# Two layers' modulation sums, on VectorE, ScalarE and GpSimd instead of in 32-column fp32 matmuls

## The reference, cut to what matters

```python
mod   = silu(c)     @ ada_w + ada_b        # ada_w is (2048, 6144): shift, scale, gate
mod_c = silu(c_ctx) @ ada_w + ada_b
h  = rms_norm(x)   * (1 + scale)   + shift
hc = rms_norm(ctx) * (1 + scale_c) + shift_c
y, yc = mixer(h, hc)
x = x + gate * y;  ctx = ctx + gate_c * yc
```

## Time and profile before

| | us |
|---|---|
| median of 3 runs | 2321.89 (2319.16 to 2322.77) |
| profiled execution, first to last instruction (span) | 2319.5 |
| what lies around the span, median less span | 2.4 |
| PE busy in the span | 2153.6 (93%) |
| DVE, ACT, POOL busy | 1113.6, 712.6, 332.6 |
| PE idle in the heads of 250 to 1000 us | none that a row shows |

### The profile page before, as it was taken

One profiled execution on the slowest core, in us unless ns is written; L12 is line 12 of the kernel. 1 busy time (PEld: TensorE's weight loads), 2 busy tenths in 40 slices (PEclk: granted clock), 3 DMA queues, 4 the chain that ended last, 5 costly groups with the idle time before them and its releaser, 6 DMA issues.

```text
span 2319.5 us, 30093 instructions
## 1 busy us (share of the span) xinstructions
PE 2153.6 (93%) x11100; PEld 1706.1 (74%) x11100; DVE 1113.6 (48%) x1572; ACT 712.6 (31%) x908; POOL 332.6 (14%) x367
## 2 busy tenths in 40 slices
PE   4679999999999999989997999999999999999897
PEld 1257777777777777767885788788878787787776
DVE  1043222333322232233227777677767777778344
ACT  2042222222222222223224333233333333335333
POOL 0040000000000000001110122122221222221101
PEclk8779999999999999999998999999999999999999
DMA  8965555555555555514443535554455445355654
GB/s 345 346 168 153 164 157 155 148 156 163 161 152 148 148 154 163 145 36 125 118 119 91 152 98 139 130 141 109 127 149 128 120 122 149 102 133 167 228 182 145
DMA packets 395182, 350.15 MB, mean 151 GB/s; under 512 B 9252, under 2 KB 358020, under 8 KB 383624
## 3 DMA queue, kind: packets, MB, share of 16 engines
q1 hardware_dynamic: 380592, 267.66, 40.4%
q0 software_dynamic: 11328, 75.50, 11.6%
q10 hardware_dynamic: 3224, 6.47, 0.8%
HBM read 345.26 MB, written 4.33 MB: 151 GB/s over the span
## 4 chain that ended last, share of the span: by engine, by line
PE 64%; issue 12%; DVE 11%; DMA 6%; ACT 2%; SPq 1%; POOL 1%; DVEq 1%; ACTq 0%; POOLq 0%
PE bank L326 16%; PE bank L330 16%; PE bank L328 16%; PE bank L345 4%; DVE arena L1188 4%; DMA arena<-in_na_ada_w_dram 3%; DVE w_lo L312 3%; PE bank L1663 2%; PE bank L1664 2%; PE bank L1665 2%; DMA arena<-cs_scr 2%; PE bank L1450 1%; DVE arena L1185 1%; PE bank L1474 1%; PE bank L1593 1%
## 5 line engine op out<-in xcount | busy, mean ns | idle before, releaser
L326 PE MATMUL bank<-act_hi,w_hi 128*128 128x512 f32 (+1 forms) x2576 | 961.1, 373 | 46.7 <-DVE w_lo L312 26.8
L330 PE MATMUL bank<-act_hi,w_lo 128*128 128x512 f32 (+1 forms) x2576 | 941.7, 366 | 0.0
L328 PE MATMUL bank<-act_lo,w_hi 128*128 128x512 f32 (+1 forms) x2576 | 941.4, 365 | 0.0
L312 DVE TENSOR_TENSOR w_lo<-arena,w_hi 128x2048 fp32r<-128x2048 f32 x193 | 444.0, 2301 | 624.6 <-ACT w_hi L752 477.4
L326 PEld LDWEIGHTS bank<-act_hi,w_hi 128*128 128x128 f32 x2576 | 490.6, 190 | 169.6 <-issue 55.6
L330 PEld LDWEIGHTS bank<-act_hi,w_lo 128*128 128x128 f32 x2576 | 490.2, 190 | 79.0
L328 PEld LDWEIGHTS bank<-act_lo,w_hi 128*128 128x128 f32 x2576 | 491.3, 191 | 73.2
L308 ACT ACTIVATE w_hi<-arena 128x2048 fp32r<-128x2048 f32 x145 | 276.5, 1907 | 106.9 <-PE bank L1665 86.8
L602 POOL TENSOR_TENSOR arena<-arena 128x512 f32<-128x512 f32 (+1 forms) x128 | 137.4, 1106 | 470.7 <-ACT arena L826 470.7
L1188 DVE SCALAR_TENSOR_TENSOR arena<-arena,convc 128x512 f32<-128x512 f32 (+1 forms) x192 | 155.2, 808 | 25.4 <-DVE arena L1185 1.3
L1663 PE MATMUL bank<-w_hi,act_hi 128*128 128x512 f32 x256 | 101.8, 398 | 11.7 <-DVE w_lo L312 8.3
(11 more groups left out here) (201 smaller groups left out, 1694.1 us busy)
## 6 DMA issues: line engine op xcount, KB each, us to landing
arena<-in_ssd_w_in_dram SPq DMA_DIRECT2D x81, 1024.0 KB, 6.1
arena<-in_na_w_in_dram SPq DMA_DIRECT2D x64, 1024.0 KB, 7.6
arena<-in_ssd_ada_w_dram POOLq DMA_DIRECT2D x48, 1024.0 KB, 5.3
arena<-in_na_ada_w_dram SPq DMA_DIRECT2D x16, 2048.0 KB, 8.7
arena<-in_ssd_w_out_dram SPq DMA_DIRECT2D x32, 1024.0 KB, 5.1
arena<-in_na_ada_w_dram POOLq DMA_DIRECT2D x16, 1024.0 KB, 5.3
arena<-in_na_w_out_dram SPq DMA_DIRECT2D x16, 1024.0 KB, 6.3
arena<-cs_scr SPq DMA_DIRECT2D x64, 256.0 KB, 5.9
```

The costliest lines, as they stand in the source:

```text
L312: nc.vector.tensor_tensor(w_lo[:, n0 % 2, :], raw[slot], w_hi[:, n0 % 2, :].bitcast(F32), ALU.subtract).then_inc(s_lo, 1)
L326: nc.tensor.matmul(bank[b][:, 0:cols], w_hi[:, b, w], act_hi3[:, k, 0:cols], start=(k == 0), stop=False)
L328: nc.tensor.matmul(bank[b][:, 0:cols], w_hi[:, b, w], act_lo3[:, k, 0:cols], start=False, stop=False)
L330: mm = nc.tensor.matmul(bank[b][:, 0:cols], w_lo[:, b, w], act_hi3[:, k, 0:cols], start=False, stop=(k == KT - 1))
```

## The change

The same sums in another layout. Head i now takes 512 columns (for heads 0 to 3 the first layer's gate, for 4 to 15 the second layer's three vectors) and all 2048 rows, in eight parts of two row blocks each (128 partitions x 2 x 512, 512 KB), which GpSimd loads into two buffers. VectorE multiplies each block by c's column and adds it up in `ada_acc`. ScalarE multiplies each block by c_ctx's column into `ada_prod`, two blocks to a part, and GpSimd adds these up in `acc`. A head later VectorE turns both sums in 32x32 blocks and reduces them to 16 columns each of bank 2. After the last head, bank 2 is copied, and four matmuls with the selector `sel4` (four identities of 32 added up) add the four partition groups. The matmuls of `add_modulation` go, `cond_slot` with them. The gate row, now with its bias, goes to DRAM in one DMA of 4-byte elements behind the second output tile; the bias broadcast and its addition at the end go.

```diff
-            def load_ada(v, i):
+            def load_ada(l, i, gate):
...
-                    pool.wait_ge(s_gused, i * 4 + v)
+                    pool.wait_ge(s_gd, i * 8 + (l - 1))
+                    pool.wait_ge(s_ga, i * 8 + (l - 1))
...
-                w, at = (na_ada_w, 2 * D) if v == 0 else (ssd_ada_w, (v - 1) * D)
-                rows = w[0:P, at:at + D] if i is None else w[bass.ds(i * P, P), at:at + D]
-                pool.dma_start(ada_rows, rows).then_inc(s_gin, 16)
-
-            load_ada(0, None)
+                elif l >= 2:
+                    pool.wait_ge(s_gd, l - 1)
+                    pool.wait_ge(s_ga, l - 1)
+                if gate:
+                    at = 2 * D if i is None else i * 512 + 2 * D
+                    w = na_ada_w
+                else:
+                    at = i * 512 - D
+                    w = ssd_ada_w
+                rows = w.rearrange("(k p) n -> p k n", p=P)[:, 2 * l:2 * l + 2, bass.ds(at, 512)]
+                pool.dma_start(ada_buf[l % 2], rows).then_inc(s_gin[l % 2], 16)
+
...
+            def add_products(l, i, base=0):
+
+                pool.wait_ge(s_ga, l + 1 if i is None else i * 8 + (8 * base + l + 1))
+                if l == 0:
+                    if i is not None:
+                        pool.wait_ge(s_gred, i * 1)
+                    nc.gpsimd.tensor_tensor(acc[:, :], ada_prod[:, 0, :], ada_prod[:, 1, :], ALU.add)\
+                      .then_inc(s_gp, 2)
+                    return
+                for h in range(2):
+                    n = 2 * l + h
+                    pool.wait_ge(s_gp, n if i is None else i * 16 + (16 * base + n))
+                    nc.gpsimd.tensor_tensor(acc[:, :], acc[:, :], ada_prod[:, h, :], ALU.add).then_inc(s_gp, 1)
+
...
+            load_ada(0, None, True)
+            load_ada(1, None, True)
...
             head_bias(None)
-            for v in range(1, 4):
-                load_ada(v, None)
-            with pool.Fori(1, HEADS) as i:
-                load_ada(0, i)
+            add_products(0, None)
+            for l in range(2, 8):
+                load_ada(l, None, True)
+                add_products(l - 1, None)
+
+            def head_sums(i, gate):
+                load_ada(0, i, gate)
+                add_products(7, i, -1)
+                load_ada(1, i, gate)
                 head_bias(i)
-                for v in range(1, 4):
-                    load_ada(v, i)
+                add_products(0, i)
+                for l in range(2, 8):
+                    load_ada(l, i, gate)
+                    add_products(l - 1, i)
+
+            with pool.Fori(1, 4) as i:
+                head_sums(i, True)
+            with pool.Fori(4, HEADS) as i:
+                head_sums(i, False)
+            add_products(7, HEADS - 1)
+            pool.wait_ge(s_gred, HEADS)
+            nc.gpsimd.memset(acc[:, :], 0.0).then_inc(s_acc, 1)
...
-            pool.wait_ge(s_gsp, 64)
-            pool.dma_start(gate_b, gate_scr.rearrange("(o a) b -> o (a b)", o=1).broadcast_to([P, D]))\
-                .then_inc(s_gb, 16)
-            pool.wait_ge(s_ylo, 32)
-            pool.dma_start(bias_b, ssd_ada_b[2 * D:3 * D].rearrange("(o d) -> o d", o=1).broadcast_to([P, D]))\
-                .then_inc(s_gb, 16)
-            pool.wait_ge(s_gb, 32)
-            nc.gpsimd.tensor_tensor(gate_b, gate_b, bias_b, ALU.add).then_inc(s_gbr, 1)
+            pool.wait_ge(s_gsp, 16)
+            pool.dma_start(gate_b, gate_scr.broadcast_to([P, D])).then_inc(s_gbr, 16)
             pool.wait_ge(s_yr0, 1)
             pool.dma_start(fn_b, final_norm_w.rearrange("(o d) -> o d", o=1).broadcast_to([P, D]))\
                 .then_inc(s_gb, 16)
-            pool.wait_ge(s_gb, 48)
+            pool.wait_ge(s_gb, 16)
...
+            def products(l, t8):
+
+                act.wait_ge(s_gin[l % 2], 16 * (l // 2 + 1) if t8.i is None else t8.i * 64 + 16 * (l // 2 + 1))
+                if t8.i is not None or l > 0:
+                    act.wait_ge(s_gp, 2 * l if t8.i is None else t8.i * 16 + 2 * l)
+                for h in range(2):
+                    k = 2 * l + h
+                    m = nc.scalar.activation(ada_prod[:, h, :], ada_buf[l % 2][:, h, :], ACT.Copy,
+                                             scale=cond_c[:, k, 1:2])
+                m.then_inc(s_ga, 1)
...
+                if first:
+                    act.wait_ge(s_h, KT)
+                products(0, t1)
                 act.wait_ge(s_used, t4.at(1))
                 nc.scalar.activation(q_t, backwards(bank[0][:, :]), ACT.Copy, scale=QSCALE)\
...
                 next_hi(2, t4)
                 if not first:
                     turned_probs(Turn(t1.i, 1, -1))
+                for l in range(1, 4):
+                    products(l, t1)
                 act.wait_ge(s_used, t4.at(2))
                 nc.scalar.activation(k_t, bank[1][:, :], ACT.Copy).then_inc(s_free[1], 1)
                 next_hi(3, t4)
+                for l in range(4, 6):
+                    products(l, t1)
                 act.wait_ge(s_used, t4.at(3))
                 nc.scalar.activation(v_t, bank[0][:, :], ACT.Copy).then_inc(s_free[0], 1)
                 next_hi(4, t4)
+                for l in range(6, 8):
+                    products(l, t1)
...
-            act.wait_ge(s_gused, 4 * HEADS)
-            nc.scalar.activation(mod_rows, bank[2][:, :], ACT.Copy).then_inc(s_grow, 1)
...
-
-            act.wait_ge(s_grow, 1)
-            for j in range(4):
-                act.dma_start(gate_scr[j:j + 1, :], mod_rows[32 * j + 6:32 * j + 7, :]).then_inc(s_gsp, 16)
...
             for u in range(2):
                 out_tile(u, Turn(), None)
+            act.wait_ge(s_mod2, 1)
+            act.dma_start(gate_scr.rearrange("o (k p) -> p (o k)", p=P), mod_s[:, 2, 0, :],
+                          allow_slow_non_contiguous=True).then_inc(s_gsp, 16)
...
+            step(nc.vector.tensor_tensor(sel4[:, :], ident[:, 0:32], ident[:, 32:64], ALU.add))
+            for q in range(2, 4):
+                step.wait()
+                m = nc.vector.tensor_tensor(sel4[:, :], sel4[:, :], ident[:, 32 * q:32 * q + 32], ALU.add)
+                if q == 2:
+                    step(m)
+            m.then_inc(s_sel, 1)
...
+            def ada_part(l, t8):
+
+                first = t8.i is None
+                dve.wait_ge(s_gin[l % 2], 16 * (l // 2 + 1) if first else t8.i * 64 + 16 * (l // 2 + 1))
+                for h in range(2):
+                    k = 2 * l + h
+                    if k == 0:
+                        m = nc.vector.tensor_scalar(ada_acc, ada_buf[0][:, 0, :], cond_c[:, 0, 0:1], None, ALU.mult)
+                    else:
+                        if h == 1:
+                            step.wait()
+                        else:
+                            dve.wait_ge(s_gd, l if first else t8.i * 8 + l)
+                        m = nc.vector.scalar_tensor_tensor(ada_acc, ada_buf[l % 2][:, h, :], cond_c[:, k, 0:1],
+                                                           ada_acc, ALU.mult, ALU.add)
+                    if h == 0:
+                        step(m)
+                m.then_inc(s_gd, 1)
+
+            def ada_sums(t8):
+
+                dve.wait_ge(s_gd, t8.at(8))
+                dve.wait_ge(s_gp, Turn(t8.i, 16, 2 * t8.base).at(16))
+                h = t8.i - 1 if t8.i is not None else HEADS - 1
+                for s, a in ((0, ada_acc), (1, acc[:, :])):
+                    step(nc.vector.transpose(z_th, a))
+                    step.wait()
+                    dst = bank[2][:, 32 * h + 16 * s:32 * h + 16 * s + 16] if t8.i is None else \
+                        bank[2][:, bass.ds(h * 32 + 16 * s, 16)]
+                    m = nc.vector.tensor_reduce(dst, z_th.rearrange("p (c j) -> p c j", j=32), AX.X, ALU.add)
+                    if s == 0:
+                        step(m)
+                        step.wait()
+                m.then_inc(s_gred, 1)
...
+            def ada_columns(v, s, dst, ada_bias):
+
+                src = bank[3][:, 32 * v:32 * v + 32].rearrange("p (i s m) -> p i s m", s=2, m=4)[:, :, s, :]
+                return nc.vector.tensor_tensor(dst.rearrange("p (i m) -> p i m", m=4), src,
+                                               ada_bias.rearrange("p (i m) -> p i m", m=4), ALU.add)
...
-                    dve.wait_ge(s_gused, i * 4)
-                for v in range(4):
-                    m = nc.vector.tensor_copy(cond_slot[:, 34 * v:34 * v + 2], cond_c[:, 0, :] if first else
-                                              cond_c[:, bass.ds(i * 1, 1), :].rearrange("p a s -> p (a s)"))
-                m.then_inc(s_gslot, 1)
-                if not first:
                     normalise(l3)
+                    ada_sums(Turn(i, 8, -8))
+                if first:
+                    dve.wait_ge(s_h, KT)
+                ada_part(0, t1)
                 split_lo(dve, 2, t4, 2)
                 if not first:
                     dve.wait_ge(s_pt, l1.at(1))
```

(36 more changed lines are left out.)

29 lines of the change are left out of this document (14 added, 15 removed).

## The result

The changed kernel takes 2270.85 us (median of 4, 2269.67 to 2272.36), the one before 2322.33 (2319.16 to 2328.63); the ratio is 0.978, 95% interval 0.977 to 0.980. Predicted were 2261, range 2243 to 2300. The profiled execution after took 2272.36, its span is 2270.7.

The account below looks back on a forecast made before the run. TensorE was taken to bound the heads, the sums' chain nearly so; -63 - 5.5 + 7 + 4.2 + 0.5 - 0.5 - 4.0 = -61.3 us from span 2319.5 gives 2258.2, plus 2.4: 2261 us, range 2243 to 2300.

Parts of the forecast that it names:

- Removal, -63: TensorE in 15 heads: without the groups of four 32-column products each head loses about 4.2 us, together -63 us.
- 3 x 0.08: TensorE in a head: the step before a removed group is 0.08 us wider in three of four places.
- Lateness, +7: Heads: the tanh comes late, 3 us from the first head plus 14 x 0.3, +7 us; bounds 0 and +35.
- The chain's length: Sums' chain through ScalarE, GpSimd and VectorE in one head: 52.1 us from the tanh, 1 us later than due.
- The room before product 1: Start of the chain in a head: 0.7 us of room, 16.8 with the hand-over against 17.5; then lateness grows 0.3 per head.
- The slack of 3.7 us: TensorE before turning the probabilities: covers a late tanh by 4.7 us, 3.7 after the removal.
- The landing of 5.0 us given to every part: Loads of 512 KB parts in the heads: each taken to land in 5.0 us, bounds 3 and 7.7.
- The upper bound, two slower landings a head: Heads: each load 1 us slower at the two places where the chain waits for one, lateness up to +35 us.
- First head, -5.5: First head: 15 us lost with two groups and slow clock, 9.5 returned by a late weight split, net -5.5 us.
- Behind the last head, +4.2: TensorE's wait behind the last head: VectorE's transposes, reductions and sums copy stand in between, +4.2 us; bounds 2.5 and 10.
- End, -4.0: Output stage: without the bias broadcast (2.6) and its GpSimd addition (1.4), -4.0 us; bounds 0 and -9.5.
- A: Rival: the chain bounds the heads, 2 us longer than forecast; 2291 us, +30, range 2275 to 2316, chance 0.22.

Follow-up runs that it names:

- e1: The changed kernel with the sums in the heads left out altogether (no ada loads, products, additions or turning); 15 head periods took 758.6 us, 50.57 us each.
- e3: The changed kernel without VectorE's own sum except for row block 0; 15 head periods took 782.5 us, against 783.3 in the changed kernel.
- e9: The changed kernel with part 2's load issued ahead of the first addition in GpSimd's program, in every head; 2245.8 us, 15 head periods 759.6.
- e10: The changed kernel with every part's load moved ahead of the two additions before it in GpSimd's program; 2391.5 us, 15 head periods 893.5.

## Why the prediction was right, and which terms were off

- **Removal, -63.** Measured -71.8 (e1): 4.79 us a head, not 4.2. The groups' own 3.98 us were right (starts of all matmuls of 12 heads, averaged). Mis-sized was the term for the neighbours, 3 x 0.08: the matmuls around the four groups lose 0.81 us in all, 0.28 in the step of L1478, 0.27 in L1465 and L1502, the rest in the scores and the projection. I had read it off the starts of groups and missed what the last matmul ahead of a group pays.
- **Lateness, +7.** Measured 24.7 in the heads alone, by the starts against e1: 12.9 us more before the turning of the probabilities, 9.5 before projections. The chain's length was right, 52.1 us from tanh to tanh: it is 52.3 on average. Two steps in it failed.
  - *The room before product 1.* The additions of part 0 were to end at 16.7 us, with 0.7 us of room, so that only 0.3 us of lateness is handed on. Beside the split they end at 18.6 and ScalarE waits for them: there is no room, and a head hands on all of its lateness. The first head leaves the tanh 3.3 us late (3 predicted), the next ones 3.8 to 4.6. The slack of 3.7 us was right, 4.6 less 0.9 of waiting, but it is used up from the second head on.
  - *The landing of 5.0 us given to every part.* Part 2's is 7.5 because a 1 MB tile is issued just ahead of it, and the prediction didn't lay these two issues side by side. Product 3 then ends at 32.0, not 29.8, though part 3's load is issued 22.8 us behind the tanh, where I had 23.0. What follows is quicker than predicted and makes up for most of it: product 7 ends at 51.2 us in the head shown (50.8 predicted).

  Every head pays 1.65 us instead of 0.3. The upper bound, two slower landings a head, was in the range; the named places were parts 3 and 6, and it was part 2.
- **First head, -5.5.** Measured -5.1; the wait 7.91 us against 7.5, and slow matmuls behind it as said. Its two halves hold too: -14.1 without sums (15 predicted), 9.0 given back (9.5).
- **Behind the last head, +4.2.** The wait grew by 4.0 us. The stage grew by 2.4, the small matmuls having left it, and the stretch after it by 1.1; the experiments except e1 took 210.2 to 212.1 us there, against 212.2. The later store and loads stayed hidden.
- **End, -4.0.** Measured -3.6; the wait 7.50 became 3.42 and both splits 2.29.
- **Sum and rivals.** A's form, a slower landing, is what happened, 17.7 us more than my lateness where A had 30. The undersized removal, -8.8, hid half of it. The two errors aren't independent: while the chain sets the period, what TensorE needs less comes back as waiting (worked out from the rows, no run shows it). So a head is 52.2 us where the sum has 51.6, and that the total is within 10 us is partly luck. By stretches, measured less predicted: heads +8.9, first head +0.4, behind the last head -0.7, SSD projections +4.5, in front of the output +0.4, output +0.4, start -1.4: +12.5, the span of 2270.7 against 2258.2.
- **The port.** On the rule of the Trainium skill, "SBUF — State Buffer", section "SBUF: two separate sides": the trace agrees that an addition beside a split takes 3.34 us and not 1.30. Its meetings with VectorE's sum decide little: with that gone the heads take 782.5 (e3). Its meeting with the split is what holds the first addition until the tile is issued, by the rows in nine of the 14 heads; no run takes that away by itself. The box on the "DVE blocks DMA" trap on the same page of the Trainium skill is about VectorE's 2-port perf-mode operations, and the section "Who interferes with whom" there says that `tensor_tensor`, which the split is, was not seen to stall a DMA. The trace agrees: the load at 605.24 in e9 is issued 0.9 us into a 3.10-us split and lands in 4.0 us, like the others.

## What to carry to other kernels

When a sum's operands are streamed by an engine that also computes, write down for each load what is issued just ahead of it on the other queues and what it stands behind in its own; a load behind work that can only end after the event that releases a big tile comes second. Put an issue where its engine would wait anyway: here one load moved ahead of one addition gave 24 us in the heads (e9), and every load moved ahead of the additions for which the next engine waits cost 110 (e10). And price a removed small matmul group with its neighbours.

## What the runs showed of the hardware

A 512 KB load lands in 4.0 us ahead of a 1 MB load and in 7.1 to 8.5 when issued 0.9 us behind one; at 2.3 us behind, 5.2 to 5.9. An addition of 128x512 on GpSimd that starts beside VectorE's split of 128x2048 ends 1.15 us behind the split's end, in ten heads of the changed kernel. The gate's store of 4-byte elements in the changed kernel stood beside a 1 MB tile load that landed only after 15.5 us, where others there take 6.3; 3.45 us of ScalarE's wait came of it and none of TensorE's:

```profile
1015.28 0.47 ACTq L830 DMA_DIRECT2D gate_scr<-mod_s  x1
...
1031.02 1.92 ACT L310 ACTIVATE w_hi<-arena 128x2048 fp32r<-128x2048 f32 x1 [3.45 <-DMA arena<-in_na_w_out_dram]
```
